# Attention scores made twice, once for the row maximum and once with keys on partitions, in a hybrid encoder step

## What is computed

```
F_all = cumsum(concat(logf_prev, logf))
s = einsum('bqhd,bkhd->bhqk', qi, kf) * scale
s = s + (F_q[..., :, None] - F_k[..., None, :])
s = where(k_pos <= q_pos, s, NEG_BIG)
p = softmax(s, axis=-1)
o = einsum('bhqk,bkhd->bqhd', p, vf)
```

## Time and profile before

| | us |
|---|---|
| median of 3 runs | 3280.39 |
| span of the profiled execution | 3280.3 |
| attention, first score to last output | 773.8 |
| PE busy in the span | 2472.3 (75%) |
| DVE | 1555.6 (47%) |
| ScalarE | 1133.4 (35%) |
| GpSimd | 289.4 (9%) |

### The profile page before, as it was taken

One profiled execution on the slowest core, in us unless ns is written; L12 is line 12 of the kernel. 1 busy time (PEld: TensorE's weight loads), 2 busy tenths in 40 slices (PEclk: granted clock), 3 DMA queues, 4 the chain that ended last, 5 costly groups with the idle time before them and its releaser, 6 DMA issues. The chain is left out here.

```text
span 3280.3 us, 39435 instructions
## 1 busy us (share of the span) xinstructions
PE 2472.3 (75%) x12634; PEld 1975.0 (60%) x12635; DVE 1555.6 (47%) x2832; ACT 1133.4 (35%) x2069; POOL 289.4 (9%) x300
## 2 busy tenths in 40 slices
PE   7779999729996376776767739980999999999600
PEld 1168888629995254554555528860788778888500
DVE  0258888730101255554646636653134562344458
ACT  0144444312222244443545534321123442234422
POOL 0000000000000000000000000004111211112123
PEclk9889999859998688787878869995999999999855
DMA  6621111144463712133330054432245663444576
GB/s 240 235 77 67 67 67 61 42 140 154 158 201 120 170 43 62 38 70 71 70 70 1 7 157 146 137 109 93 95 141 179 212 237 128 141 157 170 204 249 221
DMA packets 220659, 410.64 MB, mean 125 GB/s; under 512 B 45240, under 2 KB 109014, under 8 KB 217372
## 3 DMA queue, kind: packets, MB, share of 16 engines
q1 hardware_dynamic: 201740, 355.76, 34.3%
q0 software_dynamic: 18832, 53.90, 4.7%
HBM read 293.14 MB, written 116.47 MB: 125 GB/s over the span
## 5 line engine op out<-in xcount | busy, mean ns | idle before, releaser
L1191 PE MATMUL c_pt<-ident,c_pr 128*128 128x128 f32 x1128 | 214.1, 315 | 140.1 <-DVE c_pt_lo L1314 70.7
L1314 DVE TENSOR_TENSOR c_pt_lo<-c_pt,c_pt_hi 128x512 fp32r<-128x512 f32 (+2 forms) x360 | 203.8, 574 | 219.6 <-ACT c_pt_hi L1280 218.5
L1191 PEld LDWEIGHTS c_pt<-ident,c_pr 128*128 128x128 f32 x1128 | 146.8, 158 | 219.6 <-DVE c_pt_lo L1314 132.0
L1273 ACT ACTIVATE c_pr<-c_ps,c_nm 128x1024 f32<-128x1024 f32 (+7 forms) x200 | 171.1, 859 | 257.2 <-DVE c_nm L1303 143.1
L1280 ACT ACTIVATE c_pt_hi<-c_pt 128x512 fp32r<-128x512 f32 (+2 forms) x360 | 176.5, 503 | 151.9 <-PE c_pt L1191 151.5
L1227 PE MATMUL c_ps<-c_k,c_q 68*128 68x512 f32 (+1 forms) x336 | 152.9, 455 | 87.2 <-ACT c_pr L1273 43.7
L267 PE MATMUL b_ps<-b_h_hi,wb_hi 128*128 128x256 f32 x576 | 165.2, 287 | 52.2 <-DMA b_h_lo<-h_lo 52.2
L1043 DVE TENSOR_TENSOR b_qk_lo<-b_qk,b_qk_hi 128x2048 fp32r<-128x2048 f32 x11 | 25.2, 2293 | 334.0 <-ACT b_qk_hi L997 334.0
L1206 PE MATMUL c_po<-c_pt_hi,c_vv 128*128 128x512 f32 (+2 forms) x360 | 165.2, 459 | 20.2 <-DVE c_pt_lo L1314 20.2
L269 PE MATMUL b_ps<-b_h_hi,wb_lo 128*128 128x256 f32 x576 | 164.4, 285 | 0.0
L268 PE MATMUL b_ps<-b_h_lo,wb_hi 128*128 128x256 f32 x576 | 164.3, 285 | 0.0
(11 more groups left out here) (353 smaller groups left out, 6110.4 us busy)
## 6 DMA issues: line engine op xcount, KB each, us to landing
x_raw_g<-in_w_gate_dram SPq DMA_DIRECT2D x32, 1024.0 KB, 7.3
x_raw_u<-in_w_up_dram SPq DMA_DIRECT2D x32, 1024.0 KB, 9.8
x_raw_d<-in_w_down_dram SPq DMA_DIRECT2D x32, 1024.0 KB, 6.3
wa<-in_w_ada_dram SPq DMA_DIRECT2D x12, 2048.0 KB, 7.7
z_y<-y_tok SPq DMA_DIRECT2D x32, 512.0 KB, 5.0
v_hl<-b_v_hl SPq DMA_DIRECT2D x21, 512.0 KB
c_k<-k_hi SPq DMA_DIRECT2D x16, 672.0 KB
h_hi<-ah_hi SPq DMA_DIRECT2D x17, 512.0 KB, 2.6
```

The source lines that it names most:

```text
L1191: last = pe.transpose(p_t[i % 2][:, j * P:(j + 1) * P], pr[:, it["chunk"] % 2, j, it["kb"] * P:(it["kb"] + 1) * P], c.ident[:])
L1273: act.activation(pr[:, u["chunk"] % 2, u["j"], h0 * P:(h0 + nk) * P], p_s[hf % 2][:, 0:nk * P], ACT.Exp, bias=nm[:, n:n + 1], accum_out=su ...
L1314: dve.tensor_tensor(pt_lo[:, n % 3, cols], p_t[n % 2][:, cols], pt_hi[:, n % 3, cols].bitcast(F32), ALU.subtract).then_inc(lo_done, 1)
```

## The change

Scores are made twice. Once with queries on partitions, for the row maximum alone, from one float32r product (q_hi with k_hi and the two rows -F_hi, -F_lo of the key, tile km) in pieces of 4 key tiles (p_m); DVE reduces each piece. The maxima of a chunk's units are put on a diagonal (dg), multiplied by ones on PE and so broadcast as a row (p_x), from which one partition is copied into row 96 of q2. The second time with keys on partitions, item by item, from k1, q1 and k2, q2, where the row with the negated maximum and rows of zeros and ones lie in q2 and k2. ScalarE takes exp with -F of the key as a bias per partition (nf) straight into the layout that the product with V needs; the transposes are gone. ScalarE then rounds pr to pr_hi, DVE subtracts to pr_lo, both out of SBUF. GpSimd adds pr of every item of a chunk into acc, for the denominator. At the end of a chunk PE multiplies ot by a folding matrix and acc by ones, in float32, into p_x. F of the query is no longer added, since it falls out of the softmax. Rings of three tiles (p_s, pr, pr_hi, pr_lo) replace the large pr. `forget_sums` stores two rows instead of eight and turns -F into a tile neg_f on the chip.

The core of the diff:

```diff
@@ forget_sums
-            sp.wait_ge(ones_set, 1)
-            for r in range(2):
-                sp.dma_start(c.f_k[:, r, :], ones[:]).then_inc(stored, 16)
-                sp.dma_start(c.f_q[:, 2 + r, :], ones[:, 0:TP]).then_inc(stored, 16)
-            sp.wait_ge(lo_ready, 3)
-            sp.dma_start(c.f_q[:, 0, :], hi[:, 0:TP].bitcast(F32)).then_inc(stored, 16)
-            sp.dma_start(c.f_q[:, 1, :], lo[:, 0:TP].bitcast(F32)).then_inc(stored, 16)
-            sp.dma_start(c.f_k[:, 2, :], nhi[:]).then_inc(stored, 16)
-            sp.dma_start(c.f_k[:, 3, :], nlo[:]).then_inc(stored, 16)
-            sp.wait_ge(stored, 16 * 8)
+            sp.wait_ge(lo_ready, 1)
+            sp.dma_start(c.f_k[:, 0, :], hi[:].bitcast(F32)).then_inc(stored, 16)
+            sp.dma_start(c.f_k[:, 1, :], lo[:].bitcast(F32)).then_inc(stored, 16)
+            sp.wait_ge(stored, 16 * 2)
...
+            pe.wait_ge(neg_ready, 1)
+            for t in range(NT_K):
+                last = pe.transpose(ps_f[:, t * H:(t + 1) * H], F[:, t * P:(t + 1) * P], c.ident[0:H, 0:H])
+            last.then_inc(f_T, 1)
...
+            dve.tensor_scalar(F[:], F[:], -1.0, None, ALU.mult).then_inc(neg_ready, 1)
+            dve.wait_ge(neg_ready, 1)
-            dve.tensor_scalar(nhi[:], hi[:].bitcast(F32), -1.0, None, ALU.mult).then_inc(lo_ready, 1)
-            dve.wait_ge(lo_ready, 1)
-            dve.tensor_scalar(nlo[:], lo[:].bitcast(F32), -1.0, None, ALU.mult).then_inc(lo_ready, 1)
+            dve.wait_ge(f_T, 1)
+            dve.tensor_copy(c.neg_f[:].rearrange("p h t -> p t h"), ps_f[:].rearrange("p (t h) -> p t h", h=H))
@@ attention
+            begin, length = (rounds[ci - 1]["items"][0], rounds[ci - 1]["items"][-1] + 1) if ci else (-4, 0)
+            length -= begin
+            todo = [x for u in r["units"] for x in units[u]["pieces"]]
+            for n, x in enumerate(todo):
+                events.append((begin + 0.6 * n * length / len(todo) + piece_lag, "piece", x))
+            events.append((begin + 0.6 * length + row_lag, "row", ci))
+            events.append((begin + 0.6 * length + row_lag + 0.2, "row_out", ci))
...
+        pr, pr_hi, pr_lo = sb("pr", [P, RING, 512]), sb("pr_hi", [P, RING, 512], F32R), sb("pr_lo", [P, RING, 512], F32R)
+        acc, fold = sb("acc", [P, 2, 512]), sb("fold", [P, HD])
...
+        p_m = [ctx.enter_context(nc.psum_tensor(f"c_pm{i}", [P, 512], F32)) for i in range(2)]
+        p_s = [ctx.enter_context(nc.psum_tensor(f"c_ps{i}", [P, 512], F32)) for i in range(NPS)]
         p_o = [ctx.enter_context(nc.psum_tensor(f"c_po{i}", [P, 512], F32)) for i in range(2)]
+        p_x = ctx.enter_context(nc.psum_tensor("c_px", [P, 512], F32))
...
+                for dst, src in ((raw(q2[0:HD, s]), c.q_hi[rows]),
+                                 (raw(km[0:HD, s]), c.k_hi[rows]), (raw(km[HD:, s]), c.f_k[head].rearrange("o r t -> (o r) t")),
+                                 (raw(q1[0:HD, s]), c.q_hi[rows]), (raw(q1[HD:P, s]), c.q_lo[rows]),
...
+        @block.gpsimd
...
+                    cols = columns(it)
+                    total = acc[:, it["chunk"] % 2, cols]
+                    wait(pool, exp_done, m, n)
+                    if it["first"]:
+                        wait(pool, or_T, m, it["chunk"] - 2)
+                        pool.sem_inc(acc_go, 1)
+                        pool.tensor_copy(total, pr[:, n % RING, cols]).then_inc(summed, 1)
+                    else:
+                        wait(pool, summed, m, n - 1)
+                        pool.tensor_tensor(total, total, pr[:, n % RING, cols], ALU.add).then_inc(summed, 1)
...
-            def turn(m, i):
+            def piece(m, x):
+                pc = pieces[x]
+                u = units[pc["unit"]]
+                s = u["s"]
+                if u["chunk"] % (NCH // 2) == 0 and u["j"] == 0 and pc["x"] == 0:
+                    pe.wait_ge(loaded[s], m * (16 * N_LOADS) + 16 * N_LOADS)
+                wait(pe, mx_done, m, x - 2)
+                d = u["diag"] - pc["h0"]
+                w = pc["nk"]
+                kc = slice(u["k0"] + pc["h0"] * P, u["k0"] + (pc["h0"] + w) * P)
+                masked = 0 <= d < w
+                last = pe.matmul(p_m[x % 2][:, 0:w * P], q2[0:KR, s, u["tile"] * P:(u["tile"] + 1) * P], km[:, s, kc], start=True, stop=not masked)
+                if masked:
+                    last = pe.matmul(p_m[x % 2][:, d * P:(d + 1) * P], ident_r[:], neg_qk_r[:], start=False, stop=True)
+                last.then_inc(m_done, 1)
...
+                wait(pe, exp_done, m, i - NPS)
+                out = p_s[i % NPS]
+                pe.matmul(out[:, cols], k1[:, s, kc], q1[:, s, qc], start=True, stop=False)
+                if it["diag"] is not None:
+                    d = it["diag"]
+                    pe.matmul(out[:, d * P:(d + 1) * P], ident_r[:], neg_ts_r[:], start=False, stop=False)
                 if it["first"]:
+                    wait(pe, row_ready, m, it["chunk"])
+                pe.matmul(out[:, cols], k2[0:ROW + 1, s, kc], q2[0:ROW + 1, s, qc], start=False, stop=True).then_inc(s_done, 1)
...
             def times_v(m, i):
...
+                    wait(pe, ot_out, m, it["chunk"] - 2)
                 wait(pe, lo_done, m, i)
+                parts = [(p_o[it["chunk"] % 2][:, cols], vv[:, it["s"], kt, :], pr_hi[:, i % RING, cols]),
+                         (p_o[it["chunk"] % 2][0:HD, cols], vv[:, it["s"], kt, 0:HD], pr_lo[:, i % RING, cols])]
...
+                for what, n in schedule(0.0, 1.0, 1.3):
+                    if what == "piece":
+                        piece(m, n)
+                    elif what == "row":
+                        w = rounds[n]["n"] * P
+                        wait(pe, dg_ready, m, n)
+                        wait(pe, emptied[0], m, emptied[1])
+                        emptied = (row_ready, n)
+                        row_of = n
+                        pe.matmul(p_x[:, 0:w], ones_r[:], dg[:].rearrange("p j t -> p (j t)")[:, 0:w], start=True, stop=True).then_inc(row_done, 1)
                     elif what == "item":
+                        while ahead < min(n + 3, NI) and items[ahead]["chunk"] <= row_of:
+                            scores(m, ahead)
+                            ahead += 1
                         times_v(m, n)
                     elif what == "finish":
                         wait(pe, ot_out, m, n)
+                        wait(pe, emptied[0], m, emptied[1])
+                        emptied = (o_ready, n)
+                        wait(pe, summed, m, rounds[n]["items"][-1])
                         for j in range(rounds[n]["n"]):
+                            qs = slice(j * P, (j + 1) * P)
+                            pe.matmul(p_x[:, j * P:j * P + HD], ot[:, qs], fold[:], start=True, stop=True)
+                            last = pe.matmul(p_x[:, j * P + HD:j * P + HD + 2], acc[:, n % 2, qs], c.ones[:, 0:2], start=True, stop=True)
                         last.then_inc(or_T, 1)
...
+                        wait(act, s_done, m, n)
+                        wait(act, lo_done, m, n - RING)
+                        wait(act, summed, m, n - RING)
+                        kt = key_tile(it)
+                        act.activation(pr[:, n % RING, cols], p_s[n % NPS][:, cols], ACT.Exp, bias=nf[:, it["s"], kt:kt + 1]).then_inc(exp_done, 1)
+                    elif what == "round":
+                        cols = columns(items[n])
+                        wait(act, exp_done, m, n)
+                        wait(act, pv_done, m, n - RING)
+                        act.activation(pr_hi[:, n % RING, cols], pr[:, n % RING, cols], ACT.Copy).then_inc(hi_done, 1)
...
+                for what, n in schedule(0.1, 0.9, 1.6):
+                    if what == "piece":
+                        pc = pieces[n]
+                        u = units[pc["unit"]]
+                        many = len(u["pieces"]) > 1
+                        unit = pc["unit"]
+                        wait(dve, m_done, m, n)
+                        dve.tensor_reduce(mx[:, unit, pc["x"]:pc["x"] + 1] if many else nm[:, unit:unit + 1], p_m[n % 2][:, 0:pc["nk"] * P],
+                                          AX.X, ALU.max, negate=not many).then_inc(mx_done, 1)
+                        if n == u["pieces"][-1]:
+                            if many:
+                                wait(dve, mx_done, m, n)
+                                dve.tensor_reduce(nm[:, unit:unit + 1], mx[:, unit, 0:len(u["pieces"])], AX.X, ALU.max, negate=True).then_inc(nm_ready, 1)
+                            else:
+                                wait(dve, mx_done, m, n)
+                                dve.sem_inc(nm_ready, 1)
+                    elif what == "round":
+                        cols = columns(items[n])
                         wait(dve, hi_done, m, n)
+                        wait(dve, pv_done, m, n - RING)
```

(65 more changed lines are left out.)

198 lines of the change are left out of this document (58 added, 140 removed).

## The result

The changed kernel takes 3586.22 us (median of 4 runs, 3582.7 to 3587.71) where the kernel before, beside it, takes 3282.68 (4 runs, 3274.97 to 3285.56): ratio 1.0925, 95% interval 1.0907 to 1.0944. It is 304 us slower; the forecast was 170 slower. The profiled execution took 3587.71 us, its span is 3586.2.

The account below looks back on a forecast made before the run. No engine is full in the attention stage; they wait for each other. DVE 494 + piece waits 134 + GpSimd hold 171 + chunk ends 52 + 20 + start and turns 72 = 943 against 773.8: +170, 3450 us, range 3290 to 3580.

Parts of the forecast that it names:

- The wait for pieces: DVE waits for PE's piece behind products with V: 16 per head at 1.05 us (bounds 0 and 1.75), 134 us.
- The third rival: Whole kernel: waits push PE to its lower clock, each of 128 costs 1.75 us; +90, 3540 us, chance 0.18.
- chunk 2 has such gaps today and 0.86 of the clock: Chunk 2 in the kernel before: argument given against (c), which was to decide where PE's gaps exceed 2 us.
- (c): The third rival, by its letter; its sign was granted clocks near 0.6 in chunks 1 and 2.
- The finish: Chunk ends: PE's 8 fp32 products replace 4 transposes; booked at nothing, uncovered about 1 us per chunk, 40 us.
- The hold by GpSimd: SBUF: GpSimd's addition and DVE's subtraction take turns, 1.86 us per full item where uncovered; 21.4 per head, 171 us.
- the second rival: Whole kernel: pieces wait as said, subtraction and addition rarely collide; 812 us stage, 3318 us, chance 0.16.
- The tails: Chunk tails without pieces: GpSimd's hold on DVE costs 4.2 us in chunk 2, 1.8 in chunk 1, 1 each in others.
- DVE's own work: Attention stage: DVE's instructions sum to 494 us, 61.7 per head, 64 more than before.
- The first rival: Whole kernel: pieces always ready, additions fall beside reductions; 678 us stage, -96, 3184 us, chance 0.17.
- The fourth: Whole kernel: transposes are not on the path and nothing replaces their time; 3280 us, chance 0.02.
- Outside the stage: Head loads about +3.5 us, memsets hidden, forget_sums up to -4; together booked at 0.

Follow-up runs that it names:

- the repeats: Changed kernel with the first score product made four times over in chunks 0 to 2, the repeats overwritten: 3492.16 us.
- the one that reads PSUM: Changed kernel with DVE's lower-half instruction reading p_s in PSUM instead of pr in SBUF, maximum instead of difference, additions kept: 3538.22 us.
- pieces earlier and PE at the upper level: Changed kernel with piece products half an item earlier on PE and three repeats of the first score product in chunks 0 to 2: 3431.9 us.
- four edits: Changed kernel with pieces half an item earlier, no GpSimd additions, float32r ot and fold, and three score-product repeats in chunks 0 to 2: 3318.41 us.
- pieces earlier: Changed kernel with PE's piece products listed half an item earlier (lag -0.5 instead of 0): 3490.57 us.
- a like trick: Kernel before, with one overwritten 512-column product ahead of each item's transposes in chunks 0 to 2: 3298.49 us, ratio 1.0062.

## Why the prediction was right and wrong

The direction was right, the time 136 us too low and 6 above the range.

- **The wait for pieces** came where it was said (16 per head; 132 waits for L1222 against 128). With the 56 for L1224, which ends a piece too, it came more often: 188 waits and 280 us, against 134 us booked. Its size was the failing step. "I take 1.05" chose the upper level; the trace has 1.74, the upper bound given (1.75). The third rival priced that at 90 us, and the repeats gave back 94. Its consequence was right, its condition was not: it was to hold where PE's gaps exceed 2 us, with a gap of 1.9 expected. In the rows PE stands 0.70 us per item and is granted 0.50, where the kernel before stands up to 2.1 us at once in chunk 2 and is granted 0.86. So "chunk 2 has such gaps today and 0.86 of the clock" was no reason against it. The sign given for (c), clocks near 0.6 in chunks 1 and 2, did show (0.50), and chunk 2 took 40.1 us for the 31 to 34 of the forecast.
- **The finish** was "booked at nothing, behind the second item of the next chunk". That is the second failing step. It stands in PE's program between items, DVE's reciprocal waits for it ahead of its next subtraction, and each float32 product is two instructions. The cost "uncovered about 1 us per chunk, 40 us" was also low: 3.3 us of PE per chunk end of four tiles at the lower level; its products with fold made cheap, it gave 35.5 us back, doubled it cost 114.
- **The hold by GpSimd** is real, and chunk 3 took 30.3 us for the "about 30" forecast. But what the hold costs is 46 us of the stage by the run with no additions and 47 by the one that reads PSUM, not 171: a third term mis-sized. The subtraction takes 0.90 us on the mean, not "well above 1", since the addition has a head start, which only the second rival counted. Two rows of chunk 3, from the timelines of GpSimd and DVE:

```profile
1216.31 1.28 POOL L1205 TENSOR_TENSOR c_acc<-c_acc,c_pr 128x512 f32<-128x512 f32 x1 [3.04 <-ACT c_pr L1312]
...
1216.92 1.21 DVE L1348 TENSOR_TENSOR c_pr_lo<-c_pr,c_pr_hi 128x512 fp32r<-128x512 f32 x1 [1.20 <-ACT c_pr_hi L1317]
```

  The addition began 0.61 us earlier, and the subtraction is 0.52 us longer, where taking turns was to add 1.17. From 1219.45 us on, three additions stand in 4.65 us and three subtractions beside them in 4.03, so an item costs about 1.5 us there and not the plain sum of 1.86. Of chunk 3's growth from 17.9 us, 6.7 would be there without additions (24.6). In that run ScalarE is busy 19.2 of the 24.6 us, and chunk 2's finish holds PE 3.3 us; ScalarE's 1.3 us per item stood in the first two rivals and not in the forecast. The tails booked at 8 us per head don't show: chunks 1 and 2 are the same without additions. Chunk 3 came out at 30 by luck: one term was too large and others absent.
- **The account does not close by two steps.** With the hold booked some 125 us too high, not 136 us were missing elsewhere but about 260 (an estimate). The clock's 94 and at most 114 for the finish name some 210 of them; the rest, about 50, no run divides. It may lie in the waits that came more often than booked and in chunk 3's pace.
- **DVE's own work**: 473.8 us busy in the stage with no additions, against 494 booked. The row copy took 0.697 us for the 0.69 assumed.
- **The first rival** (faster, if pieces are always ready) has no run that meets its condition: with pieces earlier and PE at the upper level reductions still wait 108 us for PE, and the time is 3432. **The second** (3318) is, by chance of numbers alone, what four edits give; additions and subtraction do collide. **The third** had the right consequence and fell 46 us short; it too booked the finish at nothing and the hold at 171. **The fourth** is out.
- **Outside the stage** 0 was booked; the first score started 0.4 us later, and the rest of the span differs by 6 us (1390.6 and 1397.0 behind the stage), part of which other runs with the same values don't show (1391.5 with pieces earlier). The memsets of the constants stayed hidden.

## What to carry to other kernels

Where one engine waits for the other in turns, price PE's part of the loop at its lower level unless the row shows the upper one in that very pattern; here PE was busy 84% of a stretch by its records and at half its clock. A short "tail" in the order of an in-order engine is not hidden by the items around it: count its instructions (two for a float32 product) and look who stands behind them on each queue. Adding up single experiments told the causes, but their prices shift with each other (the additions cost 46 us of the stage or 90): run them together before saying what is left. And where an experiment changes values, look whether a later stage depends on them before taking the whole difference for the edit's.

## What the runs showed of the hardware that was not expected

- Work that nothing reads made the kernel 94 us faster, by taking PE's granted clock in chunk 2 from 0.50 to 0.95. In the kernel before, a like trick brought the clock from 0.87 to 1.00 and cost 0.6%.
- A float32 product with 64 or 2 moving columns is two matmul instructions, busy 0.40 or 0.33 us each on the mean of the stage; in float32r the one with 64 columns is a single instruction of 0.34. Sixteen of the float32 ones held PE for 3.3 us at the lower level.
- DVE with one input in PSUM wasn't slowed by GpSimd (687 ns beside the additions, 689 with none, 896 with both inputs in SBUF beside them), and GpSimd's own addition of 128x512 became only a little shorter by it (1278 against 1351 ns).
